# Five gate projections by one level of Strassen's algorithm in a fused encoder layer

## The reference

```python
xn = rms_norm(x) * norm_g
h  = xn @ w_in     # columns: qa ka va ua qi ki wi qb kb vb ub ga gb; ga and gb have 1024 columns each
A  = sparse attention(qa, ka, va; a top-k of an indexer's scores picks the keys), 8 heads of 64
B  = stick-breaking attention(qb, kb, vb), 8 heads of 64
ya = (A * silu(ua)) @ w_a_out          # 512 -> 1024
yb = (B * silu(ub)) @ w_b_out          # 512 -> 1024
y  = x + (sigmoid(ga) * ya + sigmoid(gb) * yb) @ w_o
```

## Time and profile before

| | |
|---|---|
| median of three runs | 528.16 us |
| profiled execution, span from first to last instruction | 527.0 us |
| PE busy | 522.5 us (99%), 4248 matmuls |
| DVE, ACT, POOL busy | 324.8 us (62%), 239.8 us (46%), 76.7 us (15%) |
| stretch of attention A | 284 to 367 us |
| stretch of the mixes and gates 3 to 7 | 367 to 476 us |
| loads of a gate unit, a mix unit, `res` | 1024, 512, 2176 KB; 4.9, 3.4, 7.9 us from issue to landing |

### The profile page before, as it was taken

How to read it: one execution, slowest core, us unless ns; L and a number is a source line. 1 busy time by engine, 2 the same in 40 slices (tenths; PEclk the granted TensorE clock), 3 DMA queues, 4 the chain that set the end, 5 groups by cost and what they waited for, 6 DMA issues and landing times.

```text
span 527.0 us, 10096 instructions
## 1 busy us (share of the span) xinstructions
PE 522.5 (99%) x4248; PEld 493.4 (94%) x4248; DVE 324.8 (62%) x659; ACT 239.8 (46%) x401; POOL 76.7 (15%) x73
## 2 busy tenths in 40 slices
PE   8999999999999999999999999999999999999997
PEld 7889999999998998989999889999999999999997
DVE  5778758899889989478622666851432343265331
ACT  7755764344366566773253775553232132231110
POOL 3506000014034423374000000000000000000000
PEclk9999999999999999999999999999999999999999
DMA  8623205142432412023320032011321321147311
GB/s 287 248 80 122 91 1 165 44 157 81 126 121 51 127 69 81 1 81 121 121 81 1 1 111 107 12 70 41 121 80 41 121 98 64 41 159 291 114 49 48
DMA packets 15357, 50.43 MB, mean 96 GB/s; under 512 B 2288, under 2 KB 6000, under 8 KB 11728
## 3 DMA queue, kind: packets, MB, share of 16 engines
q1 hardware_dynamic: 15168, 49.49, 27.4%
q10 hardware_dynamic: 144, 0.30, 0.2%
HBM read 42.82 MB, written 6.82 MB: 94 GB/s over the span
## 4 chain that ended last, share of the span: by engine, by line
PE 99%; DMA 1%; DVE 0%; issue 0%
PE PS L611 41%; PE PS L817 14%; PE PS L902 9%; PE PS L884 9%; PE PS L730 4%; PE PS L565 4%; PE PS L711 3%; PE PS L595 3%; PE PS L687 2%; PE PS L795 2%; PE PS L656 2%; PE PS L636 1%; PE PS L544 1%; PE PS L739 1%; PE PS L533 1%; PE PS L576 1%
## 5 line engine op out<-in xcount | busy, mean ns | idle before, releaser
L1303 DVE TENSOR_TENSOR wlo<-raw,whi 128x2048 fp32r<-128x2048 f32 (+1 forms) x36 | 76.0, 2110 | 60.6 <-ACT whi L948 59.2
L611 PE MATMUL PS<-xhi,whi 128*128 128x272 f32 x320 | 94.5, 295 | 0.0
L611 PE MATMUL PS<-xlo,whi 128*128 128x272 f32 x320 | 92.3, 288 | 0.0
L611 PE MATMUL PS<-xhi,wlo 128*128 128x272 f32 x320 | 92.1, 288 | 0.0
L948 ACT ACTIVATE whi<-raw 128x2048 fp32r<-128x2048 f32 (+1 forms) x36 | 61.7, 1715 | 54.7 <-PE PS L817 34.1
L611 PE MATMUL PS<-whi,xhi 128*128 128x256 f32 x256 | 73.3, 286 | 0.0
L611 PE MATMUL PS<-wlo,xhi 128*128 128x256 f32 x256 | 72.3, 283 | 0.0
L611 PE MATMUL PS<-whi,xlo 128*128 128x256 f32 x256 | 71.8, 281 | 0.0
L611 PEld LDWEIGHTS PS<-xhi,whi 128*128 128x128 f32 x320 | 60.3, 188 | 2.9 <-issue 2.3
L611 PEld LDWEIGHTS PS<-xhi,wlo 128*128 128x128 f32 x320 | 60.3, 188 | 0.0
L611 PEld LDWEIGHTS PS<-xlo,whi 128*128 128x128 f32 x320 | 60.2, 188 | 0.0
(11 more groups left out here) (236 smaller groups left out, 1144.7 us busy)
## 6 DMA issues: line engine op xcount, KB each, us to landing
raw<-in_w_units SPq DMA_DIRECT2D x28, 1024.0 KB, 4.9
raw<-in_w_mixes SPq DMA_DIRECT2D x8, 512.0 KB, 3.4
stage<-in_x_kw_qi SPq DMA_DIRECT2D x7, 564.5 KB, 5.2
res<-in_x_kw_qi SPq DMA_DIRECT2D x1, 2176.0 KB, 7.9
out<-res SPq DMA_DIRECT2D x16, 136.0 KB, 1.7
out<-vals SPq DMA_DIRECT2D x2, 1024.0 KB, 6.2
out<-kT SPq DMA_DIRECT2D x1, 1088.0 KB, 9.3
out<-tm SPq DMA_DIRECT2D x1, 1024.0 KB, 8.1
```

The source lines that it names most:

```text
L611: mm = pe.matmul(out, lhsT, rhs, start=(k == 0), stop=(k == 23))
L1303: dve.tensor_tensor(wlo[:, uu % 2, 0:n], raw[:, uu % 2, 0:n], whi[:, uu % 2, 0:n].bitcast(F32), ALU.subtract).then_inc(w_lo, 1)
```

## The change

Gates 3 to 7 become units of a new kind, `fast`. Each is a product of a 2 by 2 blocked weight (two halves of the input rows, branches a and b) and a 2 by 2 blocked input (two halves of the rows, two halves of the tokens). One level of Strassen's algorithm, in the form with shared sums (Winograd's), makes it of seven products of 12 matmuls each instead of eight: 84 matmuls a gate instead of 96. Four products take sums of weight blocks, and four take sums of input blocks.

- The sums of input blocks (s1, s2, s4 and s3, each 128 by 4 by 272 float32) are made once, by POOL: four additions as soon as the group `va0` is done, three more after `va1`, three low parts after ACT's high parts (`sum_high`), and for s3 three more after the last product with the values, because s3 is put where those values lie. s3's high part then takes the place of a quarter of `xhi`.
- The sums of weight blocks (t1 to t4) are made by DVE for each fast gate (`weight_sums`: one subtraction of 1024 columns, two of 512), during the gate before it. ACT and DVE split seven blocks of 512 columns instead of four in four parts (`fast_high`, `fast_low`).
- Products that share a sum are added in PSUM. ACT copies a bank out between two of them (`taken`), and DVE adds the rest (`added`). PE waits for these copies before it writes on.
- The units stand in the order gate2, gate3 to gate7, mix0 to mix7, out0 to out3. All gates have buffers of their own. The high and low parts of the attentions' outputs are no longer made during attention A, but during the fast gates (`high_b`, `high_a`, `o_low`). The load of `res` stands after that of mix2.
- In the mixes, the units are split two ahead, out0 with mix6 and out1 with mix7, behind the split of the sum.

```diff
-for _d in range(D // P):
-    UNITS += [(f"mix{_d}", "mix")]
-    if _d + 3 < D // P:
-        UNITS += [(f"gate{_d + 3}", "gate")]
+FAST = [f"gate{d}" for d in range(3, D // P)]
+UNITS += [(n, "fast") for n in FAST]
+UNITS += [(f"mix{_d}", "mix") for _d in range(D // P)]
...
+PRODUCTS = [("p1", "b11", "x11", "a"), ("p5", "t1", "s1", "b"), ("p6", "t2", "s2", "a"), ("p3", "b22", "s4", "b"),
+            ("p7", "t3", "s3", "a"), ("p2", "b21", "x12", "c"), ("p4", "t4", "x22", "a")]
+FAST_BANKS = [{"a": 0, "b": 2, "c": 4}, {"a": 1, "b": 3, "c": 5}]
...
+            def fast_gate(i):
+                banks = FAST_BANKS[i % 2]
+                for n, form, block_, b in PRODUCTS:
+                    part = [form in p for p in PARTS].index(True)
+                    pe.wait_ge(f_lo_done, len(PARTS) * i + part + 1)
...
+                    elif n == "p6":
+                        pe.wait_ge(f_act, 4 * i + 1)
+                    elif n == "p3":
+                        pe.wait_ge(f_act, 4 * i + 2)
+                    elif n == "p7":
+                        pe.wait_ge(f_act, 4 * i + 3)
+                        if i == 0:
+                            pe.wait_ge(s3_low, 1)
...
+                    else:
+                        pe.wait_ge(f_dve, 3 * i + 2)
+                    for c in range(KC // 2):
+                        for k, (a, w) in enumerate(PASSES):
+                            mm = pe.matmul(...)
...
             turned(N_STEPS - 1, probT, pt_done, av_done, pt_out)
+            fast_high(0, 0)
...
+            for part in range(1, len(PARTS)):
+                fast_high(0, part)
+            act.wait_ge(gates_done, gates_counted(EARLY_GATES, 1))
+            act.activation(... gates[EARLY_GATES][:, 1, :] ..., ACT.Sigmoid).then_inc(gates_sig, 1)
+            act.wait_ge(s3_summed, 1)
+            act.activation(s_hi["s3"], s3_sum, ACT.Copy).then_inc(s3_high, 1)
...
+            for i in range(len(FAST)):
+                taken(i, "p1", 0, 0)
+                next_high(i, 0)
+                taken(i, "p5", 1, 1)
+                next_high(i, 1)
+                taken(i, "p6", 1, 0)
+                next_high(i, 2)
+                if i < PAIRS:
+                    high_b(i)
+                next_high(i, 3)
...
             for d in range(D // P):
                 act.wait_ge(mixed, d + 1)
+                act.activation(mhi[:, d, :], gates[d][:, 0, :], ACT.Copy).then_inc(m_hi, 1)
+                w_high(f"mix{d + 2}" if d + 2 < D // P else f"out{d + 2 - D // P}")
...
+            weight_sums(0)
+            fast_low(0, 0)
             weighed(PAIRS, av_done, av_out, 0, suA)
+            for part in range(1, len(PARTS)):
+                fast_low(0, part)
+            dve.wait_ge(s3_high, 1)
+            dve.tensor_tensor(s_lo["s3"], s3_sum, s_hi["s3"].bitcast(F32), ALU.subtract).then_inc(s3_low, 1)
+            for i in range(len(FAST)):
+                if i + 1 < len(FAST):
+                    weight_sums(i + 1)
+                next_low(i, 0)
+                next_low(i, 1)
+                added(i, "p3", 3, 1, 0)
+                next_low(i, 2)
+                added(i, "p7", 2, 1, 1)
+                if i >= 1:
+                    o_low(i - 1)
+                next_low(i, 3)
+                added(i, "p2", 1, 0, 0)
...
-            for g in POST_B + A_FILL[:5]:
+            for g in POST_B:
                 filled(g)
+            pool.wait_ge(item_done, len(ITEMS))
+            sums(high_sum, x_part("21", 0), x_part("22", 0), ALU.add)
+            link(sums(s_sum["s1"], x_part("21", 1), x_part("22", 1), ALU.add))
+            link(sums(s_sum["s1"], s_sum["s1"], high_sum, ALU.add))
+            link(sums(s_sum["s2"], s_sum["s1"], x_part("11", 0), ALU.subtract))
+            pool.sem_inc(s_summed, 1)
+            for g in A_FILL[:5]:
+                filled(g)
...
+            for k, n in enumerate(("s1", "s2", "s4")):
+                pool.wait_ge(s_high, k + 1)
+                sums(s_lo[n], s_sum[n], s_hi[n].bitcast(F32), ALU.subtract).then_inc(s_low, 1)
+            pool.wait_ge(av_done, N_STEPS)
+            pool.wait_ge(st_va, 32)
+            link(sums(s3_sum, x_part("11", 0), x_part("21", 0), ALU.subtract))
+            link(sums(s3_sum, s3_sum, x_part("11", 1), ALU.add))
+            sums(s3_sum, s3_sum, x_part("21", 1), ALU.subtract).then_inc(s3_summed, 1)
```

More of the change, by code:

```diff
@@ L193, in raw_count, with direct_index, fast_index @@
     return 16 * (u // 2 + 1)
+def direct_index(u):
+    return sum(kind != "fast" for _, kind in UNITS[:u])
+def fast_index(u):
+    return sum(kind == "fast" for _, kind in UNITS[:u])
 def sample_units(name):
@@ L1268, in _ @@
[L1268 to L1284 removed]
+                    if g != A_FILL[-1]:
+                        unit_next(g)
@@ new lines, in _, with taken, next_high @@
+            act.wait_ge(s3_summed, 1)
+            act.activation(s_hi["s3"], s3_sum, ACT.Copy).then_inc(s3_high, 1)
+            def taken(i, product, f, h):
+                act.wait_ge(f_done, len(PRODUCTS) * i + AT[product])
+                bank = ps[:, FAST_BANKS[i % 2]["b" if product == "p5" else "a"], 0:HALF_NT]
+                act.activation(gates[EARLY_GATES + 1 + i][:, f, halved(h)], bank, ACT.Copy).then_inc(f_act, 1)
+            def next_high(i, part):
+                if i + 1 < len(FAST):
+                    fast_high(i + 1, part)
+                elif part in (1, 3):
+                    w_high(f"mix{part // 2}")
@@ new lines, in next_low @@
+            def next_low(i, part):
+                if i + 1 < len(FAST):
+                    fast_low(i + 1, part)
+                elif part in (1, 3):
+                    w_low(f"mix{part // 2}")
+            for i in range(len(FAST)):
+                if i + 1 < len(FAST):
+                    weight_sums(i + 1)
[8 more added lines that the diff above has]
+                added(i, "p2", 1, 0, 0)
@@ L1725, in _ @@
+            for c in range(PAIRS, 2 * PAIRS):
+                o_low(c)
+            for d in range(D // P):
                 dve.wait_ge(mix_done, d + 1)
-                dve.wait_ge(gates_sig, gates_sigmoid(d, 1))
+                if d <= EARLY_GATES:
+                    dve.wait_ge(gates_sig, 2 * (EARLY_GATES + 1))
+                else:
+                    dve.wait_ge(f_sig, d - EARLY_GATES)
                 for f in range(2):
-                    v = by(2, gring[d % 3][:, f, :])
+                    v = by(2, gates[d][:, f, :])
@@ L1888, in laid_out @@
             units.append(by_partition(w_in[:, c:c + UC]))
+        elif kind == "fast":
+            c = P * int(name[4:])
+            a, b = (by_partition(w_in[:, k + c:k + c + P]) for k in (GA, GB))
+            units.append(np.concatenate([a[:, 0:4], b[:, 0:4], b[:, 4:8], a[:, 4:8]], axis=1).reshape(P, KC, UC))
         elif kind == "gate":
```

322 lines of the change are left out of this document (202 added, 120 removed).

## The result

The changed kernel takes 536.84 us (median of 4 runs, 536.19 to 537.02) against 528.32 us of the kernel before in the same comparison (528.13 to 528.79): ratio 1.0158, 95% interval 1.0143 to 1.0172. That is 8.5 us slower. I had forecast 531.5 us with a range of 527.0 to 535.0: the direction was right, the size was not. The profiled execution spans 535.3 us against 527.0, so the traces hold 8.3 us of the difference.

What follows compares the result with a forecast made beforehand. PE, busy 99% of the span, was taken to bound the kernel. Removed matmuls -7.5, attention A +3.9, first fast gate +5.7, other gates +0.1, mixes to output +1.2 give +3.4 us: 531.5 us, range 527.0 to 535.0.

Steps and rivals of the forecast that it cites:

- What bounds the kernel, and what is removed: PE sets the time throughout; 12 matmuls fewer in each of 5 gates, 0.1256 us each, save 7.5 us.
- The price of POOL's sums: One POOL sum of 1088 columns takes 2.12 us, at 1.76 ns a column from earlier two-input operations.
- They exclude each other: POOL's two-input operations and DVE's operations on SBUF inputs cannot overlap; the later one waits to the other's end.
- They alternate: POOL and DVE take turns: whichever waits gets in between two successive operations of the other.
- Place 1: Attention A: POOL's sums hold DVE's small operations and make PE wait, 3.9 us together, bounds 0.7 and 5.0.
- Place 2: First fast gate: s3's sums come late and delay p6 by 4.4 us; 5.7 us with later waits, bounds 3.2 and 7.1.
- The waits of 0.6 and 0.7 further on: First fast gate, after p6: p7 waits 0.6 us for ACT, p4 waits 0.7 us for DVE's additions.
- Places 3 and 4: Other fast gates: DVE and ACT work nearly fits, 0.1 us; mixes to output: out0's later split stalls PE 1.2 us.
- Rival 3: Slower by the same places, plus PE's clock falling during p6's wait, +1.7 us: 533.2 us; chance 0.17.
- Rivals 1 and 2: Faster, weaker POOL-DVE holds: 525.9 us, chance 0.13; no change, attention A costing only 0.7 us: 528.4 us, chance 0.14.
- rival 4: Later fast gates: weights' pipeline doesn't fit, 2.0 us for four gates: 533.5 us, 535 with a fallen clock; chance 0.09.

## Why the prediction was off

**What bounds the kernel, and what is removed: right.** 60 matmuls fewer, 0.1256 us each; the later fast gates took 10.63, 10.63, 10.54 and 10.56 us against 10.55.

**The price of POOL's sums: mis-sized, 2.12 us instead of 2.50 to 2.55.** I took it from the earlier trace rows, which are multiplications with a shifted second input. Nearer rows lay in the same trace: additions without a shift, of 256 columns in 0.72 us and of 512 in 1.27, in POOL's timeline of the kernel before:

```profile
47.23 1.27 POOL L1791 TENSOR_TENSOR tm<-tm,oT 32x512 f32<-32x512 f32 x1
```

That is 2.15 ns for each further column, which gives 2.51 for 1088. All thirteen operations carry this. The Trainium skill (GPSIMD Engine Reference, section 3.1) has 4497 ns for an addition of 2048 float32 columns; an estimate from it is 2.39 for 1088. It, too, was nearer than my row.

**They exclude each other: right. They alternate: right only where a semaphore stands between two sums.** Linked sums start 0.08 us after the one before has ended, and DVE got in there each time. The first two are not linked: the second started at 287.25, before the first's end at 287.29, and DVE had to let both pass. The Trainium skill (SBUF — State Buffer, "Who interferes with whom") says that whoever issues first blocks the other fully; the trace agrees, and adds that with two operations close together the one that waits may lose again (4.16 us against 1.67 when linked).

**Place 1, 3.9 forecast, 8.6 measured: the step that failed.** The stall at step 3's logits was to be 2.2, a middle between "the negation waits" (3.0) and "it doesn't" (1.2 to 2). It waits. From 3.0, longer sums make 3.75 (the gap with the first sum linked), the unlinked pair makes 5.0, and 2.45 of slow matmuls come on top, which I had considered only for p6. My upper bound of 5.0 for the whole place put longer sums, the unlinked pair and the clock at nothing. It was also too low by its own terms: stalls of 3.0, 2.1 - 1.1 = 1.0 and 1.6 are 5.6. The sum of all my upper bounds with the 5.0, 536.3 us, lies below what was measured. Between the traces the change came out 4.9 us above the forecast (8.3 against 3.4), and this place has 4.7 of them. The values' products were 0.9 and 0.5 between starts (0.8 and 0.4 in the shifts) against 0.6 and 1.1; over the whole stretch they moved PE by 1.1 against 1.7.

**Place 2, 5.7 forecast, 6.6 measured: right in mechanism, short in size.** p6's gap was 5.0 against 4.4, because s3 was summed 0.6 later than forecast. Sums of 2.54 instead of 2.12 would by themselves have made it 1.2 later; but the two turns from 374.73 to 381.62 took 6.9 us and not 2 x (2.54 + 1.22) = 7.5. The waits of 0.6 and 0.7 further on did not show behind the 18 slow matmuls (1.6 us); with the clock kept up, p4's came back, p7's did not. That the slow matmuls nearly replaced the two waits, so that the place came out close, is luck. The statement that ACT's order makes p6 wait was only half of it, as the experiment with s3's parts moved shows.

**Places 3 and 4: right,** 0.2 and 1.25 us against 0.1 and 1.2.

**The rivals.** Rival 3 named the clock, and the falls came, with granted clocks of 0.50 and 0.57 behind the two gaps; it put +1.7 on p6, where the slow matmuls took 1.6 but cost 0.3 on balance, and nothing on attention A, where they cost 2.45. Its time, 533.2, was 3.6 us short. Its chance of 0.17 was too low with one fall seen and two waits of several us forecast. Rivals 1 and 2 fell with the first trace: the holds are as the earlier trace rows show them. The pipeline of the weights fits (rival 4).

**What is open.** Why a second input a column further on makes POOL faster. And how many matmuls a fall of the clock slows: the same gap of 5.1 us ahead of p6 was followed by 18 in one trace and some 24 in another; no edit here controls it.

## What to carry to other kernels

Price a moved operation by rows of its own operand layout, and ask for each engine pair that excludes the other what stands behind the operation that is held: the same sums cost 5 us at a point where PE waits two hand-overs later, and nothing 8 us earlier. Write down every wait on PE of some microseconds twice, once for itself and once for the matmuls at half clock behind it, and strike the second where a later wait would take its place: here it cost 2.45 us in one place and 0.3 in the other. When a change has saved work but added waits, look whether each wait is one of place: here three moves of a few lines turned 1.6% slower into 1.0% faster.

## What the hardware showed that I had not expected

- A DVE operation of two columns (a negation, 0.17 us) was held for 4.16 us by POOL's operations, to within 0.03 us of their end.
- The clock fell some 5.2 us after PE had stopped at 378.35: it was granted in full over 378.00 to 383.10, while PE stood, and matmuls were at half speed from 383.6 on, 0.4 us after it had started again. In the kernel without sums it fell within the same gap (0.88 from 369.60 to 374.60), and in attention A too (0.85 from 291.00 to 296.40). After the last matmul of the kernel before I had read 2.1 us.
- POOL took 2.00 us for 1022 columns with the second input one column further on and 2.34 without, for the same number of columns.

The stretch of the kernel without sums, as the stretches of the first section:

```profile
369.60:374.60 5.00, 0.26 (x3) 0.04 (x1) 4.91 (x3) 1.44 (x3) 3.45 (x2) 0.88 0.00 0
```
